# Thirty-six products behind the last one of a two-block network, with stationary columns at several strides

## The chip, the core and the metric

The kernel runs on one core of one Trainium2 chip. The metric is the device time of one launch in microseconds. The kernel before took 952.93 us, the median of three runs (952.01, 952.93 and 953.76).

## What is computed

The reference runs 256 tokens of width 1024 through two layers of one network and one layer of another, all in F32. Each layer of the first is a mixer and a gated feed-forward part, each with a normalisation ahead of it and a sum behind it; the layer of the second has three attention branches, merged by gates, and one last product, which is all that stands near the change:

```python
for i in range(DEPTH):                      # first block, two layers
    h = rms_norm(x, norm_mix[i])
    x = x + mixer(h, ...)                   # convolution and pooling, then sparse attention
    x = x + swiglu(rms_norm(x, norm_ffn[i]), ffn_gate[i], ffn_up[i], ffn_down[i])

# second block, one layer
branches = jnp.stack([o_a * silu(ga), o_b * silu(gb), o_c * silu(gc)], axis=2)
br = jnp.einsum('bsiw,iwd->bsid', branches, w_branch)
merged = jnp.sum(sigmoid(gate_logits) * br, axis=2)
x = x + jnp.einsum('bsd,de->bse', merged, w_out)
```

## The kernel before

Weights come from HBM in tiles of 128 x 2048 F32 values (1 MB), issued by SyncE (SP) into three slots of `raw`. ScalarE rounds each tile into `whi` (line 422, type F32R) and VectorE puts what the rounding left off into `wlo` (line 445). Activations are held in the same two parts (`hhi`/`hlo`, `yhi`/`ylo`: 128 partitions, 8 chunks of 256 columns). One product of F32 values is therefore three products of F32R parts, high by high, high by low and low by high, written out in `product` (lines 464 to 467) and summed in a bank of PSUM. `ps` is PSUM, eight banks of 512 F32 columns. In a row of a profile the first operand behind the arrow is the one that moves, the second the stationary one.

Two helpers set the order in which columns are read. `halves` (line 469) takes n neighbouring columns as two halves and goes to and fro between them, so that each column is half the width away from the one before; `in_order` undoes it when the bank is read:

```python
def halves(columns):
    return columns.rearrange("p (a b) -> p b a", a=2)
```

The gate and up products of the feed-forward part (`ffn_pe`, 256 moving columns) and all products of `rows_part` (line 578, 512 moving columns) move their operand through `halves`; `mm_feature` (256 columns) and the query, key and value products of the second block (512 columns) move theirs in plain order. `place(t, n)` (line 399) is the slot of `whi` or `wlo` that holds tile n, 2048 columns wide.

TensorE (PE) takes its work in program order. The last function in its program is `blk2_pe` (line 2032), which walks an order written out beforehand. Products of the second block rotate through banks 5 to 7 (`bank`, line 2007); `RELEASED` lists, for every use of a bank, the semaphore and the count that tell that ScalarE or VectorE has emptied it. Behind the walk come four tiles of `w_out_2`: for each, PE waits for the tile's low part and for the merged activations, and `mm_rows` (line 600) adds 2 x 2 pieces of 128 tokens x 512 columns into banks 0 to 3, with `yhi`/`ylo` as stationary operand for the first two tiles and `hhi`/`hlo`, chunks 4 to 7, for the last two.

The end of the kernel stands behind that. VectorE adds each finished bank to `x` (line 747). SP stores the first 128 tokens in one DMA (line 2511) and the others in two (line 2514), each as soon as its addition is done, and then waits until all three have landed. Last, every engine drains and a barrier joins all of them; these closing instructions carry line 134. At the start of the kernel PE runs 18 products of a constant tile, plain F32, into bank 7, which nobody reads (line 2695).

Of the kernel before, what the change touches and what calls it, by code (L numbers as in the profile page):

```python
# [21 lines left out]
P = 128  # L22
T = 256
# [108 lines left out]
def build(nc, a, out):  # L132
    ctx = ExitStack()
    with ctx:
        def sb(name, shape, dt=F32):
            return ctx.enter_context(nc.sbuf_tensor(name + "_sb", shape, dt))
# [6 lines left out]
        whi = sb("whi", [P, (SPLIT - 1) * TILE + KC * WIDE], F32R)  # L143
        wlo = sb("wlo", [P, (SPLIT - 1) * TILE + KC * WIDE], F32R)

        x = sb("x", [P, NT, D + 2])
        hhi = sb("hhi", [P, KC, T], F32R)
# [26 lines left out]
        ps = ctx.enter_context(nc.psum_tensor("ps", [P, 8, 512], F32))  # L174
# [224 lines left out]
        def place(t, n):  # L399

            at = (n - N_WIDE - 1) % SPLIT * TILE
            return t[:, at:at + (KC * WIDE if n == N_WIDE else TILE)]
# [66 lines left out]
        def halves(columns):  # L469

            return columns.rearrange("p (a b) -> p b a", a=2)
# [128 lines left out]
        def mm_rows(n, lhs_hi, lhs_lo, k0, first, last, bank=0):  # L600

            for i in range(NT):
                for h in range(2):
                    mm = rows_part(n, lhs_hi, lhs_lo, k0, i, h, first, last, bank)
            return mm
# [1315 lines left out]
        for items, u in segments:  # L1921
# [41 lines left out]
            if u is not None:  # L1963
# [7 lines left out]
                start = JOB_START[u]  # L1971
# [17 lines left out]
                if u == 3:  # L1989
                    k = body.index(("finish", 1))  # L1990
# [9 lines left out]
        N_OUT2 = N_B2 + len(b2_tiles)  # L2000
# [6 lines left out]
        def bank(use):  # L2007
            return 5 + use % 3
# [3 lines left out]
        RELEASED, counts = [], {"emptied": 0, "turned": 0}  # L2012
# [19 lines left out]
        def blk2_pe(pe):  # L2032
            for e in order:
# [64 lines left out]
                elif e[0] == "branch":  # L2098
                    _, b, use = e
                    pe.wait_ge(o_gated, 2 * b + 2)  # L2100
                    for f in range(2):
                        wait_use(pe, use + f)
                        for c in range(2):
                            for i in range(NT):
                                mm = nc.tensor.transpose(
                                    ps[:, bank(use + f), c * T + i * P:c * T + (i + 1) * P],
                                    ob[:, BR_OB[b], i, (2 * f + c) * P:(2 * f + c + 1) * P], ident[:, :])
                        mm.then_inc(b_T, 1)
            for r in range(4):
# [2 lines left out]
                mh, ml = (yhi, ylo) if r < 2 else (hhi, hlo)  # L2112
                mm_rows(N_OUT2 + r, mh, ml, 2 * r + (4 if r < 2 else 0), r == 0, r == 3).then_inc(tile_used, 1)

        BR_OB = (0, 1, 0)

        def qk_index(item):
# [656 lines left out]
```

## Time and profile before

| | |
|---|---|
| median of three runs | 952.93 us (952.01 to 953.76) |
| the profiled execution | 954.75 us |
| its span, first to last instruction | 953.0 us |
| PE busy | 940.2 us (99%), 7053 products |
| PE weight loads | 852.7 us (89%) |
| VectorE busy | 612.3 us (64%) |
| ScalarE busy | 490.8 us (52%) |
| GpSimd busy | 213.7 us (22%) |
| mean granted clock of PE | 0.998 |

The profile is of one execution; its span leaves out what lies ahead of the first instruction and behind the last. PE and its weight loads (PEld) are shown apart, and both overlap: consecutive products start closer together than the time that each of them is shown with, so the distance from start to start is the rate. "q" behind an engine's name marks its queue: waits, drains and DMA issues, which count as no busy time.

### The profile page before, as it was taken

What the parts mean: (1) busy time and instruction counts of PE and PEld (TensorE: products, weight loads), DVE (VectorE), ACT (ScalarE), POOL (GpSimd) and SP (SyncE); (2) the same over time, 40 slices, a digit from 0 to 9 for tenths busy, and PEclk for the clock granted to TensorE, in tenths of its full rate; (3) what the DMA queues carried; (4) which work ended last, traced back from release to release, by engine and by line L of the source; (5) the groups of instructions that cost most, each with busy time, mean ns of one, the idle gap of its engine ahead of it and who ended that gap; (6) DMA issues with size and microseconds to landing.
All of it is one profiled execution on the core that took longest, in us unless ns stands there. A gap on an engine that the chain in (4) does not pass through costs nothing.

```text
span 953.0 us, 17117 instructions
## 1 busy us (share of the span) xinstructions
PE 940.2 (99%) x7053; PEld 852.7 (89%) x7053; DVE 612.3 (64%) x827; ACT 490.8 (52%) x729; POOL 213.7 (22%) x177
## 2 busy tenths in 40 slices
PE   9999999999999998999999999999999999999998
PEld 8999999999889897899999987778787878999997
DVE  5866554545589898764545457756665755946754
ACT  6346444444554565744344446455555555646452
POOL 0005980000032130000000002216472505910100
PEclk9999999999999999999999999999999999999999
DMA  8665856566555512466666574536554525663461
GB/s 275 218 217 164 285 186 210 186 208 205 176 190 169 186 46 89 133 221 191 207 188 208 191 246 147 195 119 207 155 190 126 194 94 175 203 195 98 138 208 45
DMA packets 119636, 168.75 MB, mean 177 GB/s; under 512 B 5556, under 2 KB 88596, under 8 KB 119572
## 3 DMA queue, kind: packets, MB, share of 16 engines
q1 hardware_dynamic: 119140, 167.66, 55.0%
q8 instruction: 45, 0.74, 0.3%
q10 hardware_dynamic: 432, 0.19, 0.1%
q14 instruction: 19, 0.16, 0.1%
HBM read 165.38 MB, written 2.46 MB: 176 GB/s over the span
## 4 chain that ended last, share of the span: by engine, by line
PE 90%; DVE 5%; ACT 2%; POOL 1%; issue 1%; ACTq 0%; DVEq 0%; POOLq 0%
PE ps L465 25%; PE ps L467 24%; PE ps L466 24%; PE ps L923 2%; PE ps L936 2%; DVE wlo_sb L445 2%; PE ps L909 2%; POOL b_inv_sb L2472 1%; PE ps L561 1%; PE ps L734 1%; ACT whi_sb L422 1%; PE ps L500 1%; PE ps L2695 1%; PE ps L574 1%; PE ps L2094 1%
## 5 line engine op out<-in xcount | busy, mean ns | idle before, releaser
L445 DVE TENSOR_TENSOR wlo_sb<-raw_sb,whi_sb 128x2048 fp32r<-128x2048 f32 x143 | 332.7, 2328 | 186.0 <-ACT whi_sb L422 185.9
L422 ACT ACTIVATE whi_sb<-raw_sb 128x2048 fp32r<-128x2048 f32 x143 | 273.7, 1915 | 162.1 <-PE ps L467 145.7
L465 PE MATMUL ps<-hhi_sb,whi_sb 128*128 128x256 f32 x992 | 275.8, 278 | 0.9 <-DVE wlo_sb L445 0.5
L467 PE MATMUL ps<-hhi_sb,wlo_sb 128*128 128x256 f32 x992 | 274.3, 277 | 0.0
L466 PE MATMUL ps<-hlo_sb,whi_sb 128*128 128x256 f32 x992 | 274.3, 276 | 0.0
L465 PEld LDWEIGHTS ps<-hhi_sb,whi_sb 128*128 128x128 f32 x992 | 189.0, 190 | 2.7 <-issue 1.2
L466 PEld LDWEIGHTS ps<-hlo_sb,whi_sb 128*128 128x128 f32 x992 | 189.0, 191 | 0.6
L467 PEld LDWEIGHTS ps<-hhi_sb,wlo_sb 128*128 128x128 f32 x992 | 189.0, 191 | 0.0
L465 PE MATMUL ps<-whi_sb,hhi_sb 128*128 128x512 f32 (+2 forms) x304 | 119.4, 393 | 0.3 <-DVE qkl_sb L2358 0.2
L467 PE MATMUL ps<-whi_sb,hlo_sb 128*128 128x512 f32 (+2 forms) x304 | 116.5, 383 | 0.0
L466 PE MATMUL ps<-wlo_sb,hhi_sb 128*128 128x512 f32 (+2 forms) x304 | 116.4, 383 | 0.0
L465 PE MATMUL ps<-whi_sb,yhi_sb 128*128 128x512 f32 x256 | 97.9, 382 | 1.5 <-DVE wlo_sb L445 0.8
L466 PE MATMUL ps<-wlo_sb,yhi_sb 128*128 128x512 f32 x256 | 97.0, 379 | 0.0
L467 PE MATMUL ps<-whi_sb,ylo_sb 128*128 128x512 f32 x256 | 97.0, 379 | 0.0
L675 POOL TENSOR_TENSOR sinv_sb<-ssum_sb,nhalf_sb 128x1 f32<-128x1 f32 x10 | 6.4, 636 | 387.0 <-ACT scratch_sb L629 386.7
L465 PEld LDWEIGHTS ps<-whi_sb,hhi_sb 128*128 128x128 f32 x304 | 57.2, 188 | 12.8 <-DVE qkl_sb L2358 0.7
L467 PEld LDWEIGHTS ps<-whi_sb,hlo_sb 128*128 128x128 f32 x304 | 57.1, 188 | 12.0
L466 PEld LDWEIGHTS ps<-wlo_sb,hhi_sb 128*128 128x128 f32 x304 | 57.2, 188 | 10.6
L2472 POOL TENSOR_TENSOR b_inv_sb<-b_ss_sb,nhalf_sb 128x16 f32<-128x16 f32 (+1 forms) x10 | 47.5, 4748 | 68.9 <-DVE b_ss_sb L2319 68.9
L465 PEld LDWEIGHTS ps<-whi_sb,yhi_sb 128*128 128x128 f32 x256 | 48.4, 189 | 8.8 <-issue 1.6
L467 PEld LDWEIGHTS ps<-whi_sb,ylo_sb 128*128 128x128 f32 x256 | 48.4, 189 | 6.9
L466 PEld LDWEIGHTS ps<-wlo_sb,yhi_sb 128*128 128x128 f32 x256 | 48.5, 189 | 6.0
(335 smaller groups left out, 1356.1 us busy)
## 6 DMA issues: line engine op xcount, KB each, us to landing
raw_sb<-w_in SPq DMA_DIRECT2D x45, 1024.0 KB, 5.2
raw_sb<-ffn_gate SPq DMA_DIRECT2D x22, 1024.0 KB, 5.3
raw_sb<-ffn_up SPq DMA_DIRECT2D x22, 1024.0 KB, 5.3
raw_sb<-ffn_down SPq DMA_DIRECT2D x22, 1024.0 KB, 5.0
raw_sb<-w_in_even SPq DMA_DIRECT2D x8, 1024.0 KB, 8.4
raw_sb<-w_in_odd SPq DMA_DIRECT2D x8, 1024.0 KB, 5.2
raw_sb<-w_branch SPq DMA_DIRECT2D x6, 1024.0 KB, 5.1
scratch_sb<-bias_rows_dram SPq DMA_DIRECT2D x40, 128.0 KB, 3.2
```

The source lines that it names most:

```text
L422: nc.scalar.activation(place(whi, n0), in_raw(n0), ACT.Copy).then_inc(hi_ready, 1)
L445: nc.vector.tensor_tensor(place(wlo, n0), in_raw(n0), place(whi, n0).bitcast(F32), ALU.subtract).then_inc(lo_ready, 1)
L465: nc.tensor.matmul(dst, l_hi, r_hi, start=first, stop=False)
L466: nc.tensor.matmul(dst, l_hi, r_lo, start=False, stop=False)
L467: return nc.tensor.matmul(dst, l_lo, r_hi, start=False, stop=last)
L500: mm = nc.tensor.matmul(dst, w[:, k, c], h[:, k, :], start=(first and k == 0), stop=(last and k == KC - 1))
L561: nc.tensor.matmul(dst, hhi[:, k0 + k, tok], hi[:, k, :], start=(first and k == 0), stop=False)
L574: mm = nc.tensor.matmul(dst, hlo[:, k0 + k, tok], hi[:, k, :], start=False, stop=stop)
L909: mm = nc.tensor.matmul(ps[:, e, at:at + len(v) * P], ql if part == 2 else qh, kl if part == 1 else kh, start=(part == 0), stop=(part == 2))
L923: mm = nc.tensor.transpose(ps[:, b0 + n % 2, at:at + P], pr[:, 2 * (n % 2) + e, j * P:(j + 1) * P], ident[:, :])
L936: mm = nc.tensor.matmul(ps[q:q + HD, O_BANK, at:at + HD], pT[:, n % 2, e * len(v) + j, q:q + HD], v[j], start=(j == 0), stop=(j == len(v) ...
L2472: nc.gpsimd.tensor_tensor(b_inv[:, nq % 2, :, 0:heads], b_ss[:, nq % 2, 1, :, 0:heads], nhalf[:, 0:2 * heads].rearrange("p (i h) -> p i h" ...
```

## The change

Behind the last of the four `w_out_2` tiles, PE gets three waits, for the last three uses of banks 5 to 7, and 36 products of F32R parts, one pass each, into banks 6 and 7, which nobody reads afterwards. They use what is already on the core: the last tile's `whi` and `wlo`, and `hhi`. Twenty move the 256 columns of chunk 6 of `hhi` through `halves`, four each with 128 stationary columns of `whi` that are neighbours, or 2, 4, 8 and 16 columns apart. Four more do the same with four different runs of neighbours. Then come four pairs: 512 columns, chunks 4 and 5 of `hhi` in turns, and 256 columns of chunk 6. The last four have 128 columns of `hhi` as stationary operand and move 256 columns of `whi`. No semaphore is raised by any of them.

```diff
@@ -2112,6 +2112,22 @@
                 mh, ml = (yhi, ylo) if r < 2 else (hhi, hlo)
                 mm_rows(N_OUT2 + r, mh, ml, 2 * r + (4 if r < 2 else 0), r == 0, r == 3).then_inc(tile_used, 1)
 
+            w, wl = place(whi, N_OUT2 + 3), place(wlo, N_OUT2 + 3)
+            for k in range(1, 4):
+                pe.wait_ge(*RELEASED[-k])
+            h = halves(hhi[:, 6, :])
+            for l in (w[:, 0:P], w[:, 0:2 * P:2], w[:, 0:4 * P:4], w[:, 0:8 * P:8], w[:, 0:16 * P:16]):
+                for _ in range(4):
+                    nc.tensor.matmul(ps[:, 6, 0:T], l, h, start=True, stop=True)
+            for k in range(4):
+                nc.tensor.matmul(ps[:, 6, 0:T], w[:, k * P:(k + 1) * P], h, start=True, stop=True)
+            both = hhi[:, 4:6, :].rearrange("p k t -> p t k")
+            for k in range(4):
+                nc.tensor.matmul(ps[:, 6, :], w[:, k * P:(k + 1) * P], both, start=(k == 0), stop=(k == 3))
+                nc.tensor.matmul(ps[:, 7, 0:T], wl[:, k * P:(k + 1) * P], h, start=(k == 0), stop=(k == 3))
+            for k in range(4):
+                nc.tensor.matmul(ps[:, 6, 0:T], hhi[:, k, 0:P], halves(w[:, 0:T]), start=True, stop=True)
+
         BR_OB = (0, 1, 0)
```

## Rows read from the trace of the kernel before

**Rows 1.** The page: span, PE's busy time, shares of the last chain by engine.

```profile
span 953.0 us, 17117 instructions
...
PE 940.2 (99%) x7053; PEld 852.7 (89%) x7053; DVE 612.3 (64%) x827; ACT 490.8 (52%) x729; POOL 213.7 (22%) x177
...
PE 90%; DVE 5%; ACT 2%; POOL 1%; issue 1%; ACTq 0%; DVEq 0%; POOLq 0%
```

**Rows 2.** The timeline from 942 on, its end: start us, us, engine, line, instruction.

```profile
947.99 0.19 PEld L467 LDWEIGHTS ps<-whi_sb,hlo_sb 128*128 128x128 f32 x1
948.04 1.63 SPq L2514 DMA_DIRECT2D out<-x_sb  x2
948.20 0.38 PE L467 MATMUL ps<-whi_sb,hlo_sb 128*128 128x512 f32 x1
948.61 0.69 DVE L747 TENSOR_TENSOR x_sb<-x_sb,ps 128x512 f32<-128x512 f32 x1 [0.60 <-PE ps L467]
```

**Rows 3.** Instructions of line 134: ns min/median/max, first and last start in us.

```profile
L134 PEldq DRAIN  x1: 4075/4075/4075, 944.5 to 944.5; - x1
...
L134 SPq COMPARE_BRANCH  x1: 38/38/38, 952.6 to 952.6; - x1
L134 SPq DRAIN  x1: 13/13/13, 952.7 to 952.7; - x1
...
L134 PEldq EVENT_SEMAPHORE  x1: 51/51/51, 952.9 to 952.9; - x1
```

**Rows 4.** Waits of SP from 930 on: total us, times, longest us.

```profile
SPq L134 <- DMA out<-x_sb: 2.9, 1, 2.9
```

**Rows 5.** Timeline of 925 to 953: ScalarE's last reading of banks 5 to 7.

```profile
927.89 0.60 ACT L2228 ACTIVATE scratch_sb<-ps 128x512 f32<-128x512 f32 x1 [2.23 <-PE ps L467]
```

**Rows 6.** Timeline of the closing products: first and last of 19 in a row.

```profile
944.10 0.38 PE L466 MATMUL ps<-wlo_sb,hhi_sb 128*128 128x512 f32 x1
...
947.98 0.38 PE L466 MATMUL ps<-wlo_sb,hhi_sb 128*128 128x512 f32 x1
```

**Rows 7.** Timeline of PE in the feed-forward part: first and last of 21.

```profile
149.77 0.28 PE L465 MATMUL ps<-hhi_sb,whi_sb 128*128 128x256 f32 x1
...
152.00 0.28 PE L467 MATMUL ps<-hhi_sb,wlo_sb 128*128 128x256 f32 x1
```

**Rows 8.** Timeline of PE in the first mixer, plain order: first and last of 21.

```profile
39.83 0.28 PE L467 MATMUL ps<-hhi_sb,wlo_sb 128*128 128x256 f32 x1
...
42.18 0.28 PE L466 MATMUL ps<-hlo_sb,whi_sb 128*128 128x256 f32 x1
```

**Rows 9.** Timeline of PE in the second block, plain order: first and last of 15.

```profile
599.63 0.40 PE L467 MATMUL ps<-whi_sb,hlo_sb 128*128 128x512 f32 x1
...
602.90 0.40 PE L466 MATMUL ps<-wlo_sb,hhi_sb 128*128 128x512 f32 x1
```

**Rows 10.** Busy time by stretch: columns as in the first row.

```profile
core 0: us, PE busy (x) PEld busy (x) DVE busy (x) ACT busy (x) POOL busy (x), PEclk, DMA share, GB/s
...
940.00:948.70 8.70, 8.58 (x40) 7.18 (x38) 2.15 (x4) 0.00 (x0) 0.00 (x0) 1.00 0.13 52
```

**Rows 11.** PE's groups by line and form: count, busy us, mean ns, idle before.

```profile
L2695 PE MATMUL ps<-onesd_sb 128*128 128x128 f32 x36 | 7.1, 389 | 1.2 <-POOL onesd_sb L2524 1.2
```

**Rows 12.** Weight loads by line and form: count, busy us, mean ns, idle before.

```profile
L465 PEld LDWEIGHTS ps<-hhi_sb,whi_sb 128*128 128x128 f32 x992 | 189.0, 190 | 2.7 <-issue 1.2 <-DVE wlo_sb L445 0.8
...
L936 PEld LDWEIGHTS ps<-scratch_sb 128*64 128x64 f32 x672 | 22.2, 139 | 7.6 <-issue 5.5 <-ACT scratch_sb L964 0.3
...
L1150 PEld LDWEIGHTS ps<-scratch_sb,onesd_sb 128*128 128x128 f32 x24 | 3.5, 191 | 0.3
...
L1172 PEld LDWEIGHTS ps<-raw_sb,scratch_sb 128*32 128x32 f32 x64 | 1.7, 109 | 1.1
...
L1238 PEld LDWEIGHTS ps<-scratch_sb 128*15 128x15 f32 x8 | 0.4, 95 | 0.1
```

**Rows 13.** DMAs that write the output: time from issue to landing.

```profile
DMA to landing us min/median/max: 2.1/2.7/3.2
```

## Prediction

> **What bounds the kernel now.** First the page: TensorE (PE) is busy 99% of a span of 953.0 us and the chain that ended last is 90% PE [rows 1]. That alone would say that every product added to PE is paid in full. But the change stands behind the last product, so I read the end of the timeline next [rows 2]: the last product starts at 948.20 and takes 0.38, so PE is done at 948.58; VectorE's last addition runs from 948.61 to 949.30; the last store is issued right behind it. Then the closing instructions, line 134 [rows 3]: every engine drains, and a barrier joins them. PE's drain is entered at 944.5 and lasts 4.075 us, so it ends at 948.6, with the last product. SyncE (SP) reaches its own drain only at 952.7, because it waits 2.9 us for the last store to land [rows 4]; the barrier then runs to 953.0. So over the last 4.1 us (948.6 to 952.7) PE has nothing to do and the store sets the end. That slack is the cover of the change: PE work added behind the last product is free up to 4.1 us, and what exceeds it moves the end one for one.
>
> **The change part by part.** Nothing is removed or moved. Added are three waits and 36 products, each with its own weight load, all on PE, with no semaphore and no reader.
>
> *The waits.* They ask that the last three uses of banks 5 to 7 have been emptied. The last instruction that signals this is ScalarE's copy of line 2228, at 927.89 for 0.60 us [rows 5], 20 us before the last product, so none of them stands. Their own handling costs nothing either: PE's sequencer is at its drain 4 us before the last product ends [rows 3], so it works through waits while products queued ahead still run. Behind them on PE only the new products are queued; nobody waits for those but the closing barrier.
>
> *The products.* 28 move 256 columns in the interleaved order of `halves` (20 with stationary columns at strides 1, 2, 4, 8, 16, four each; 4 with plain neighbours; 4 with hhi as stationary); the 4 pairs move 512 columns, with the two feature chunks interleaved, and 256. Start to start, not the 0.28 or 0.38 us of a row, is the price, since rows overlap. In the closing products, 512 interleaved columns go at one per 215.6 ns (18 steps in 3.88 us [rows 6]); in the feed-forward stage, 256 interleaved columns at one per 111.5 ns (20 steps in 2.23 us [rows 7]), with stationary neighbours. So 28 x 111.5 = 3.12 us, and 4 x (215.6 + 111.5) = 1.31 us, together 4.43 us. The bound below is columns alone: 213 and 107 ns at 2.4 columns per ns (512 columns in 215.6 ns is that rate), 4.27 us. If all of them went as moving columns read in plain order do, 117.5 ns for 256 [rows 8] and 233.6 for 512 [rows 9], it would be 4.69 us. I take 4.43, because the moving operands of the change are interleaved as in rows 6 and 7. The granted clock is 1.0 up to the last product [rows 10], and the new products follow without a gap, so I take the full level, 2.4 GHz.
>
> *Each is one pass.* A product of plain F32 operands, like the 18 unread warm-up products of line 2695, leaves 36 rows [rows 11]; those of lines 465 to 467 leave one row each. The new ones have F32R operands. The 36 rows also show that unread products are run.
>
> *The stationary strides.* No row of before shows a stationary operand at a stride. Loads are recorded with 95 ns for 15 columns, 109 for 32, 139 for 64 and 191 for 128 [rows 12]: about 0.85 ns a column, 109 ns for 128, over a fixed part of some 82 ns. One load starts with every product, 111.5 ns apart, though each is recorded with 190: they overlap one another by that fixed part. So a load needs about the time in which 256 columns are moved, and there is little room: a stride that slows the load shows at once. Bound below: nothing, the strided load stays behind the product before it as the others do. Bounds above, from the recorded 190 ns: if strided loads follow one another without overlap, a product costs 190 instead of 111.5 ns; for 12 products at strides 4 to 16 that is 0.94 us, for 16 at strides 2 to 16 1.26 us. If they don't run behind the products either, 190 ns come on top of 111.5, 3.04 us for 16. I take zero, by the one pair of rows that shows an operand read with jumps: `halves` jumps 128 or 256 elements at every column and is the faster form, 215.6 against 233.6 ns for 512 columns [rows 6, 9], so a jump by itself is no cost where PE reads its moving operand.
>
> The Trainium skill (SBUF — State Buffer, section "Door 1: The DMA port swizzle") speaks against that: it says that reads are served in lines of 16 bytes, four F32 values, that full bandwidth wants at least two hits on a line, and that every crossing pays. By that rule strides 4, 8 and 16 would pay and stride 2 would not; an estimate by that page alone, half the rate for one hit where two are wanted, makes a load 220 ns and the 12 products 1.3 us dearer. For moving operands the rows disagree as far as jumps go, interleaved being faster than plain, but interleaving alternates between two runs of neighbours and a stride of 16 never comes back; no run here shows the load's side yet.
>
> *Sum.* PE ends 4.43 us later, at 948.58 + 4.43 = 953.01, 0.3 us past the 952.7 at which SP is ready now; the barrier behind it is as long as before, so the span becomes 953.3. The profiled execution took 954.75, 1.75 more than its span and 1.82 more than the median of 952.93; I carry the difference over: 954.75 + 0.3 for the profiled one, 952.93 + 0.3 = 953.2 for the median.
>
> **The rivals.**
> First, the cover is thinner without a profile. The last store lands after 3.2 us, while the others land after 2.1 and 2.7 [rows 13]. If the normal landing is one of these, PE's end is passed by 0.8 to 1.4 us instead of 0.3: 953.7 to 954.3. For it: the spread; against: it is the last one in the only trace there is.
> Second, strided loads take longer, since each column is read without its neighbours, so that they follow one another at their recorded length: 190 ns a product, 0.94 us more if strides 4 to 16 are concerned, 1.26 if 2 to 16: 954.2 to 954.5. For it: the load has no time to spare; against: the jumps of `halves` cost nothing. The page named above has this as its rule, for strides from 4 on.
> Third, and on the slower side: strided loads don't run behind the product before them. Each then costs its whole 190 ns [rows 12] on top of the 111.5: 16 products at strides 2 to 16, 3.04 us, 956.3. It decides (over 0.2%, 1.9 us) from (1.9 - 0.3) / 16 = 0.10 us a product. For it: nothing in the trace rules it out, as no strided load is there; against: the load of the last closing product starts at 947.99, 0.21 us ahead of it [rows 2], so pulling ahead is the normal course, whatever the addresses.
> Fourth, the products are dropped or cost less than the cover: 952.9. Against: the warm-up rows, and the 4.27 us that columns alone need.
>
> **How the numbers follow.** Forecast 0.60 (953.2); cover thinner 0.12 (954.0); longer loads 0.17 (954.4); unhidden loads 0.10 (956.3); dropped 0.01. 0.2% of 952.93, about what a measurement can tell from no change, is 1.9 us: 951.0 and 954.8 are the limits. The first two cases and the last lie inside; of the longer loads, whose upper end is 0.3 us short of the limit, I count 0.05 beyond; so slower 0.15, faster 0.02 (the spread of the three runs is 1.75 us), same 0.83. Range: from 952.3, the forecast less half that spread, to 955.0, which takes in both ends of the longer loads with 0.5 us for the spread; it leaves out the third rival, 0.10, and little else.
>
> **What would show it.** After: 36 more PE rows, all with one pass; the 256-column ones 0.11 us apart at every stride, pairs 0.33; PE's drain ending near 953.0 and SP's at 952.7, so that PE is the last into the barrier; a clock of 1.0 to the end; nothing changed ahead of 948. If rows at strides 4, 8 and 16 stand 0.19 us or more apart, the second rival holds; if those from stride 2 on stand 0.3 apart, the third. The forecast falls if the 36 take over 6.0 us (4.1 of cover and 1.9).

## The result and the profile after

The changed kernel took 955.45 us (median of 7 runs, 954.86 to 956.88) against 952.93 us of the kernel before in the same comparison: ratio 1.0028, 95% interval 1.0017 to 1.0039. A second comparison (`e10_after_again`, below) gave 1.0021, 1.0012 to 1.0030. Forecast were 953.2 us and a range up to 955.0: the time lies above the range.

The closing instructions of the profile after, in the columns of [rows 3], show who comes last into the barrier now:

```profile
L134 SPq DRAIN  x1: 13/13/13, 951.9 to 951.9; - x1
L134 PEldq DRAIN  x1: 2810/2810/2810, 952.0 to 952.0; - x1
```

PE's drain ends at 952.0 + 2.81 = 954.9, SP's at 951.9: the two have changed places, as the forecast said, but PE is later than the forecast 953.0 by 1.9 us. Of these, 0.3 us come from ahead of the change: the last closing product ends at 948.92 here and ended at 948.58 before. SP's waits after (line, what for, total us, times, longest us) say the same from the other side:

```profile
SPq L134 <- PEq L134: 3.2, 1, 3.2
...
SPq L134 <- DMA out<-x_sb: 1.7, 1, 1.7
```

SP waits 1.7 us for the last store (2.9 before, [rows 4]) and then 3.2 us for PE. The timeline of PE after (start us, us, engine, line, instruction, count; neighbours of one line are merged) has the added work:

```profile
948.54 0.38 PE L467 MATMUL ps<-whi_sb,hlo_sb 128*128 128x512 f32 x1
948.76 3.88 PE L2121 MATMUL ps<-hhi_sb,whi_sb 128*128 128x256 f32 x20
952.47 0.61 PE L2123 MATMUL ps<-hhi_sb,whi_sb 128*128 128x256 f32 x4
952.92 0.38 PE L2126 MATMUL ps<-hhi_sb,whi_sb 128*128 128x512 f32 x1
953.14 0.27 PE L2127 MATMUL ps<-hhi_sb,wlo_sb 128*128 128x256 f32 x1
...
954.23 0.61 PE L2129 MATMUL ps<-whi_sb,hhi_sb 128*128 128x256 f32 x4
```

The last closing product ends at 948.92, the last added one at 954.84: 5.92 us, not 4.43. All of the difference is in line 2121, the twenty with strides: 952.47 - 948.76 = 3.71 us where 20 x 111.5 ns = 2.23 were forecast, 1.48 us more. The four behind it take 0.45 (112 ns each), a pair 0.33, as forecast. The instructions of that one line (ns min/median/max) show the loads:

```profile
L2121 PEld LDWEIGHTS ps<-hhi_sb,whi_sb x20: 189/316/337, 948.5 to 952.1; 128*128 128x128 f32 x20
L2121 PE MATMUL ps<-hhi_sb,whi_sb x20: 273/385/404, 948.8 to 952.2; 128*128 128x256 f32 x20
```

189 ns is the old load [rows 12]; the median is 316. So the second rival happened, with longer loads than it had been given. The granted clock stays at 1.00 meanwhile (third column from the end; busy time by stretch, columns as in [rows 10]), so the clock has no part in it:

```profile
948.90:954.90 6.00, 5.94 (x37) 5.64 (x35) 0.69 (x1) 0.00 (x0) 0.00 (x0) 1.00 0.29 110
```

### The profile page after: what moved, and what is told of

The parts are those of the page before. It is cut to its first block, busy times and chain, and to the rows that moved or that the text cites. A ratio compares the mean times of both kernels' runs of the same rounds, so it can differ in the third digit from the quotient of the medians.

```text
span 955.1 us, 17190 instructions
## 1 busy us (share of the span) xinstructions
PE 944.7 (99%) x7089; PEld 857.1 (90%) x7089; DVE 612.3 (64%) x827; ACT 490.7 (51%) x729; POOL 216.0 (23%) x177
## 4 chain that ended last, share of the span: by engine, by line
PE 89%; DVE 5%; ACT 2%; POOL 1%; DMA 1%; issue 1%; SPq 0%; ACTq 0%; DVEq 0%
PE ps L465 24%; PE ps L467 24%; PE ps L466 24%; PE ps L923 2%; PE ps L936 2%; DVE wlo_sb L445 2%; PE ps L909 2%; POOL b_inv_sb L2488 1%; DMA raw_sb<-w_in_even 1%; PE ps L561 1%; ACT whi_sb L422 1%; PE ps L500 1%; PE ps L734 1%; PE ps L574 1%; PE ps L2094 1%
```

## Experiments

Executions of one and the same kernel differ by over 3 us here, with the granted clock (last section) and with how the kernel ends (`e8_before_again` and on). Beside the ratios, which take all of them, this table has medians of the executions recorded with a mean granted clock of 1.000, count in brackets, each against the kernel before in its own comparison.

| kernel | work behind the last closing product | ratio (95%) | clock 1.000 | before, clock 1.000 | difference |
|---|---|---|---|---|---|
| e1_neighbours | 4.43 us | 1.0002 (0.9993 to 1.0011) | 953.52 (6) | 952.84 (6) | +0.7 |
| e2_under_cover | 2.23 us | 0.9992 (0.9983 to 1.0001) | 952.06 (4) | 952.84 (6) | -0.8 |
| e6_twice | 11.85 us | 1.0080 (1.0065 to 1.0096) | 961.14 (3) | 952.84 (6) | +8.3 |
| e7_ahead | none, 5.9 us ahead of it | 1.0046 (1.0031 to 1.0062) | 957.95 (2) | 952.84 (6) | +5.1 |
| e9_four | 0.44 us | 0.9992 (0.9983 to 1.0001) | 951.97 (5) | 952.46 (6) | -0.5 |
| e10_after_again | 5.92 us | 1.0021 (1.0012 to 1.0030) | 955.14 (8) | 952.46 (6) | +2.7 |
| e11_one | 0.11 us | 0.9992 (0.9983 to 1.0000) | 951.85 (8) | 952.77 (15) | -0.9 |
| e12_ten | 1.11 us | 1.0000 (0.9991 to 1.0008) | 952.05 (4) | 952.77 (15) | -0.7 |

**e1_neighbours: the strides undone.**

```diff
-            for l in (w[:, 0:P], w[:, 0:2 * P:2], w[:, 0:4 * P:4], w[:, 0:8 * P:8], w[:, 0:16 * P:16]):
+            for l in (w[:, 0:P], w[:, P:2 * P], w[:, 2 * P:3 * P], w[:, 3 * P:4 * P], w[:, 4 * P:5 * P]):
```

> The 20 strided loads are replaced by loads of 128 neighbours (five places of the tile, four products each); everything else of the change stays. In the trace of the changed kernel the 36 products end 5.9 us after the last closing product, with 0.11 us at stride 1, 0.12 at 2 and 0.22 to 0.24 at 4, 8 and 16. Theory (strides 4 to 16 cost 12 x 0.12 us, and the store's landing leaves a cover of some 3 to 3.5 us): the 36 end 4.45 us after the last closing product, and the time falls by 1.4 to 1.5 us, to about 954.0. Rival (the strides are not what costs, the end is late for another reason, as more instructions or three waits): the time stays at 955.4. If the cover were the 4.1 us that the forecast read: 953.2.

PE's timeline:

```profile
946.64 0.38 PE L467 MATMUL ps<-whi_sb,hlo_sb 128*128 128x512 f32 x1
946.86 2.39 PE L2121 MATMUL ps<-hhi_sb,whi_sb 128*128 128x256 f32 x20
949.09 0.61 PE L2123 MATMUL ps<-hhi_sb,whi_sb 128*128 128x256 f32 x4
...
950.84 0.61 PE L2129 MATMUL ps<-whi_sb,hhi_sb 128*128 128x256 f32 x4
```

The twenty take 949.09 - 946.86 = 2.23 us, and all 36, from the end of the last closing product (947.02) to their own (951.45), 4.43, the forecast sum to the hundredth. The ratio of 1.0002 can't be told from no change, and its interval, up to 1.0011, lies below both of the changed kernel's, from 1.0017 and 1.0012. So the strides are what made the kernel measurably slower; without them the time can't be told from the forecast, a ratio of 1.0003.

**e3_512_columns: strided loads ahead of longer products.** Four products each with strides 1, 2, 4, 8 and 16, all moving 512 interleaved columns.

```diff
+            for _ in range(4):                        # in place of the 36; the same for each stride
+                nc.tensor.matmul(ps[:, 6, :], w[:, 0:4 * P:4], both, start=True, stop=True)
```

> 20 products that move 512 interleaved columns, with stationary columns at strides 1, 2, 4, 8 and 16, four each, in place of the 36. Theory (a strided load takes 0.22 to 0.24 us but runs behind the product before it): 0.216 us from start to start at strides 1 and 2, 0.22 to 0.24 at 4 to 16. Rival (a strided load doesn't overlap the product, or adds its 0.12 us to any product): 0.33 to 0.34 us at strides 4 to 16.

The timeline, one line of the kernel for each stride:

```profile
946.88 1.03 PE L2121 MATMUL ps<-hhi_sb,whi_sb 128*128 128x512 f32 x4
947.75 1.03 PE L2123 MATMUL ps<-hhi_sb,whi_sb 128*128 128x512 f32 x4
948.61 1.11 PE L2125 MATMUL ps<-hhi_sb,whi_sb 128*128 128x512 f32 x4
949.55 1.13 PE L2127 MATMUL ps<-hhi_sb,whi_sb 128*128 128x512 f32 x4
950.52 1.08 PE L2129 MATMUL ps<-hhi_sb,whi_sb 128*128 128x512 f32 x4
```

From group to group a product costs 217 ns at stride 1, 215 at 2, 235 at 4 and 242 at 8; behind the first one at stride 16 the next starts 227 ns later. So a strided load still runs behind the product before it; the distance is the longer of the two, and ahead of 512 columns nearly all of it is hidden. The third rival of the prediction is out.

**e4_sweep: which strides, and the load by itself.** Six products each in place of the 36:

```diff
+                nc.tensor.matmul(ps[:, 6, 0:T], w[:, 0:3 * P:3], h, start=True, stop=True)      # strides 1, 2, 3, 4, 5, 6, 12, 16
+                nc.tensor.matmul(ps[:, 6, 0:HD], w[:, 0:4 * P:4], halves(hhi[:, 6, 0:HD]), start=True, stop=True)  # 1, 2, 4, 16
+                nc.tensor.matmul(ps[:, 6, 0:T], hf[:, 0:4 * P:4], halves(w[:, 0:T]), start=True, stop=True)
```

> Six products each, in place of the 36: 256 interleaved moving columns with stationary strides 1, 2, 3, 4, 5, 6, 12 and 16; then 64 moving columns with strides 1, 2, 4 and 16, so that the load alone sets the rate; then stationary columns at stride 4 from hhi instead of whi. Theory (four F32 neighbours come with one read, about 1.85 ns each, and 128 columns need 128 x stride / 4 of them up to one per column): 0.11 us at stride 1, 0.118 at 2, 0.176 at 3, 0.22 to 0.24 from 4 on, whatever the stride; with 64 moving columns the same 0.118 at 2 and 0.22 to 0.24 at 4 and 16; hhi as whi. Rival (strides that are powers of two meet one bank of the memory): 0.11 to 0.13 us at 3, 5 and 6 and more at 12 and 16 than at 4.

The timeline; lines 2121 to 2135 are strides 1, 2, 3, 4, 5, 6, 12 and 16, lines 2137 to 2143 strides 1, 2, 4 and 16 with 64 moving columns:

```profile
947.80 0.83 PE L2121 MATMUL ps<-hhi_sb,whi_sb 128*128 128x256 f32 x6
948.47 0.88 PE L2123 MATMUL ps<-hhi_sb,whi_sb 128*128 128x256 f32 x6
949.18 1.21 PE L2125 MATMUL ps<-hhi_sb,whi_sb 128*128 128x256 f32 x6
950.23 1.57 PE L2127 MATMUL ps<-hhi_sb,whi_sb 128*128 128x256 f32 x6
951.64 1.52 PE L2129 MATMUL ps<-hhi_sb,whi_sb 128*128 128x256 f32 x6
953.00 1.50 PE L2131 MATMUL ps<-hhi_sb,whi_sb 128*128 128x256 f32 x6
954.33 1.77 PE L2133 MATMUL ps<-hhi_sb,whi_sb 128*128 128x256 f32 x6
955.93 1.49 PE L2135 MATMUL ps<-hhi_sb,whi_sb 128*128 128x256 f32 x6
957.26 0.75 PE L2137 MATMUL ps<-hhi_sb,whi_sb 128*128 128x64 f32 x6
957.85 0.87 PE L2139 MATMUL ps<-hhi_sb,whi_sb 128*128 128x64 f32 x6
958.55 1.58 PE L2141 MATMUL ps<-hhi_sb,whi_sb 128*128 128x64 f32 x6
959.95 1.49 PE L2143 MATMUL ps<-hhi_sb,whi_sb 128*128 128x64 f32 x6
961.25 1.75 PE L2145 MATMUL ps<-whi_sb,hhi_sb 128*128 128x256 f32 x6
```

A sixth of the distance to the next start: 112 ns at stride 1, 118 at 2, 175 at 3, 235 at 4, 227 at 5, 222 at 6, 267 at 12, 222 at 16. From stride 2 to 4 the cost follows the number of groups of four F32 neighbours that the 128 columns touch: 64 at stride 2, 96 at 3, 128 at 4, about 1.83 ns each (118 / 64 = 1.84, 175 / 96 = 1.82, 235 / 128 = 1.84). From 4 on each column has a group of its own, and the cost stays at 222 to 235 ns, powers of two or not; as strides 3, 5 and 6 pay, the rival is out. Stride 12 is out of line (267, or 2.09 a group), and why is open. That groups of four are what is read is inferred from these distances. With 64 moving columns it is 117, 233 and 217 ns at strides 2, 4 and 16, as with 256, and at stride 1 98 in the mean (31 for the first step, whose load had run behind a longer product, then 111 to 112): the load alone sets the rate. The last line has hhi at stride 4 as stationary operand; behind a first step of 374 ns its starts are 233 to 238 apart, as with whi.

**e5_moving: the same on the moving side.** 256 columns of whi at strides 1, 2, 4, 8, then 256 neighbours taken to and fro between 2, 4 and 8 parts, stationary neighbours throughout.

```diff
+                nc.tensor.matmul(ps[:, 6, 0:T], w[:, 0:P], w[:, 0:4 * T:4], start=True, stop=True)          # strides 1, 2, 4, 8
+                nc.tensor.matmul(ps[:, 6, 0:T], w[:, 0:P], w[:, 0:T].rearrange("p (a b) -> p b a", a=8), start=True, stop=True)  # 2, 4, 8
```

> Six products each, in place of the 36, all with 128 neighbours of whi as stationary columns: 256 moving columns of whi at strides 1, 2, 4 and 8, then 256 neighbours taken as 2, 4 and 8 parts between which the order goes to and fro. Theory (the moving operand is read in the same groups of four, 1.85 ns each, but a few groups stay at hand, which is why to and fro between two parts is free): 0.118 us at stride 1, 0.24 at 2, 0.47 at 4 and 8; 0.11 in two parts. In 4 and 8 parts 0.11 if that many groups are kept, 0.47 if only two are. Rival (only stationary loads suffer from strides): 0.11 to 0.12 us throughout.

```profile
947.77 0.88 PE L2120 MATMUL ps<-whi_sb 128*128 128x256 f32 x6
948.49 1.52 PE L2122 MATMUL ps<-whi_sb 128*128 128x256 f32 x6
949.84 1.58 PE L2124 MATMUL ps<-whi_sb 128*128 128x256 f32 x6
951.23 1.49 PE L2126 MATMUL ps<-whi_sb 128*128 128x256 f32 x6
952.54 0.85 PE L2128 MATMUL ps<-whi_sb 128*128 128x256 f32 x6
953.23 1.01 PE L2130 MATMUL ps<-whi_sb 128*128 128x256 f32 x6
954.07 1.50 PE L2132 MATMUL ps<-whi_sb 128*128 128x256 f32 x6
```

120 ns at stride 1, 225 at 2, 232 at 4, 218 at 8; 115 in two parts (111 within the group), 140 in four, (1.50 - 0.40) / 5 = 220 in eight. Both theories are off: strides do cost the moving operand (the rival falls), but strides 4 and 8 cost no more than 2, half of the 0.47 us that one group of four for each column would have given. What holds for the argument of the prediction: interleaving of two parts is free, of eight parts it isn't. So jumps aren't free in general. That `halves` is free because it comes back to each group at once fits these numbers, but is argued, not shown: four parts come back too, if later, and pay a part.

**e2_under_cover, e6_twice, e7_ahead: the cover.** Twenty products with neighbours only; all 36 run twice; all 36 put ahead of the last `w_out_2` tile.

```diff
+            for k in range(20):                       # e2, in place of the 36
+                nc.tensor.matmul(ps[:, 6, 0:T], w[:, k % 16 * P:(k % 16 + 1) * P], h, start=True, stop=True)
+            for _twice in range(2):                   # e6, around the 36
+                if r == 3:                            # e7, the 36 ahead of mm_rows of the last tile
```

> Only 20 products of 256 columns with neighbours as stationary columns are left of the 36, 2.23 us of PE behind the last closing product. Theory (the last store covers some 3 us or more): the time is that of the kernel before, 952.9, within 0.2%, and PE's drain ends ahead of SP's. Rival (any work behind the last product costs its length, or longer code costs): 955.1.

> The 36 products run twice, 72 in all. Theory (beyond the cover PE is the last into the barrier and each us costs one us): 5.9 us more than the changed kernel, 961.3, with the second 36 as long as the first. Rival (the cover is used a second time, or the granted clock changes): less than 960 or more than 963.

> The same 36 products, with their waits, stand ahead of the last w_out_2 tile instead of behind it, so that no store covers them. Theory: all of their 5.9 us are paid, 952.9 + 5.9 = 958.8, and the difference to the changed kernel (955.45) is the cover, 3.4 us. Rival (there is no cover, the changed kernel is slow for its 2.5 us of strided loads alone): 955.4.

Twice the work costs 8.3 us more than before at clock 1.000, 5.6 more than once (2.7; by the medians of all executions 961.17 - 955.24 = 5.9), for 5.93 us of products: beyond the cover each us is paid. That there is cover, `e2_under_cover` shows directly: PE's drain ends at 949.4, SP's at 950.1. Subtracting what is paid from what is added gives the cover in the timed executions: 11.85 - 8.3 = 3.55, 5.92 - 2.7 = 3.2, and from e1 4.43 - 0.7 = 3.7. So it is 3.2 to 3.7 us, where the trace of before shows 4.1. `e7_ahead` pays 5.1 of its 5.9 us, and `e2_under_cover` is 0.8 below the kernel before, both 0.8 less than expected. (At clock 1.000 `e7_ahead` has two executions only.) The next experiments tell what they have in common.

**e8_before_again, e9_four, e11_one, e12_ten: the last store.** The kernel before once more, and 4, 1 and 10 products in place of the 36.

```diff
+            for k in range(4):                        # e9; one in e11, range(10) in e12
+                nc.tensor.matmul(ps[:, 6, 0:T], w[:, k * P:(k + 1) * P], halves(hhi[:, 6, :]), start=True, stop=True)
```

> The kernel before, unchanged, for a second profile of its end. In its first profile the last store landed 3.2 us after its issue, in the changed kernel's 2.0 us, though nothing of the store differs. Theory (the landing varies from one execution to the next, and 3.2 us was a late one): 2.0 to 2.7 us here, and 2.9 to 3.6 us from the end of the last product to SP's drain. Rival (products that run while the store lands make it faster): 3.2 us again, and 4.1 us to SP's drain.

> Only four products of 256 columns with neighbours are left of the 36, 0.45 us of PE behind the last closing product. In the two profiles of the kernel before, a transfer of 16 KB of instructions runs while the last store does (950.12 to 951.10 in the first) and the store lands after 3.1 to 3.2 us; in the changed kernel and all its variants so far that transfer came at 943 to 946, ahead of the stores, and the store lands after 2.0. Theory (PE's code is fetched in pieces, the piece that is due at the very end delays the last store by 1.1 us, and a few more instructions make it due earlier): the fetch comes ahead of the stores, the store lands after 2.0 us, the span is 1.1 us shorter than before, ratio 0.9988. Rival (the length of the products behind the end, not the number of instructions, decides): landing 3.1 to 3.2 us and ratio 1.0000.

> One single product of 256 columns with neighbours is left of the 36, two instructions of PE and the three waits. With four products the fetch of instructions came 3.8 us ahead of the last store's issue and the store landed after 2.0 us. Theory (any few instructions more make the last piece due while PE still works): fetch ahead of the stores, landing after 2.0 us, ratio 0.9988. Rival (one product is too few): the fetch runs beside the last store, landing 3.1 to 3.2 us, ratio 1.0000.

> Ten products of 256 columns with neighbours, 1.1 us of PE behind the last closing product, to settle the time of the earlier landing: four and twenty products both gave 0.9992 with 1.0000 still inside the interval. Theory: landing after 2.0 us, span 1.1 us shorter, ratio 0.9988, and below 1.0000 by the interval. Rival (the body of the kernel gives the 1.1 us back): 1.0000.

DMA queues while the last store lands (queue, kind, packets, MB, share; in the last row KB and us from issue to landing). The kernel before, from 949 to 953:

```profile
q1 hardware_dynamic: 280, 0.50, 33.8%
q8 instruction: 1, 0.02, 1.5%
out<-x_sb SPq DMA_DIRECT2D x1, 256.0 KB, 3.2
```

`e8_before_again`, from 948 to 951.6:

```profile
q8 instruction: 1, 0.02, 2.1%
...
out<-x_sb SPq DMA_DIRECT2D x1, 256.0 KB, 3.1
```

The changed kernel, from 948.9 to 955:

```profile
q1 hardware_dynamic: 337, 0.66, 28.4%
out<-x_sb SPq DMA_DIRECT2D x1, 256.0 KB, 2.0
```

In both profiles of the kernel before, one transfer of 16 KB of instructions runs beside the last store, which lands after 3.1 to 3.2 us. In the changed kernel, both times, and in its ten other variants no such transfer stands there, and the store lands after 2.0, with PE busy meanwhile or not (in `e7_ahead` it is idle). So `e8_before_again` has its rival's numbers (3.1 us, and 4.0 from the last product to SP's drain), but not for its rival's reason: it isn't the products that matter but where the fetch falls. In `e9_four` and `e12_ten` it starts ahead of the stores (947.4 and 945.2), in `e11_one`, against what was expected, only at 951.1, behind the landing and even behind the last instruction (949.9); the store is quick in either case.

The packets show the delay itself. From 1.67 us behind the issue of the last store on, this is left in the kernel before (951 to 953) and in the changed kernel (951.34 to 953):

```profile
q1 hardware_dynamic: 9, 0.02, 3.3%
```

```profile
DMA packets 0, 0.00 MB, mean 0 GB/s; under 512 B 0, under 2 KB 0, under 8 KB 0
```

These nine packets are 16 of the store's 256 KB. The first starts at 951.09, where the fetch (950.12 to 951.10) ends, and they run one after another to 952.1; all others are through at 951.0. In `e8_before_again` the fetch ends at 949.69 and nine such packets run from 949.68 to 950.7. So a sixteenth of the store waits for the fetch, and that is the 1.1 us.

In time the other place of the fetch is worth 0.5 to 0.9 us at clock 1.000 in the four kernels whose products the store covers (e2, e9, e11, e12), less than the 1.1 expected. Their ratios, three times 0.9992 and once 1.0000 (`e12_ten`, its rival's), don't settle it by themselves.

The spans of the timed executions, first to last instruction, tell more. At clock 1.000 the kernel before has a median span of 950.2 us in 27 executions, and so have e2, e9 and e12, whose profiles show a store that lands after 2.0. The shortest spans of e2, e9, e11 and e12 are 949.8 to 950.0; with a store 1.1 us later the kernel before would not come below 950.9, and 20 of its 27 do. So in most executions of the kernel before the last store isn't late. Instead more time passes outside the span: device time less span is 1.75 to 2.01 us in the changed kernel and in e1, e2, e6, e7, e9 and e12, and over 2.01 in 32 of 65 executions of the kernel before, up to 3.01. The one profile with a fetch behind the last instruction, that of `e11_one`, has 2.41. So the fetch seems to cost the kernel before either beside the store or behind the end; for the executions without a profile that is argued, not shown. With 0.7 us for it, `e7_ahead` adds up: 5.9 less 0.7 are 5.2, measured 5.1.

**e10_after_again: the changed kernel timed once more**, without an edit.

> The changed kernel as it is, timed again beside the kernel before on one chip, for a tighter interval. Theory (the kernel before ends with the late store, 4.1 us after its last product, and PE now ends 5.9 us after it): 1.8 us more, ratio 1.0019. Rival (the cover is the 3.0 us that a store landing after 2.0 us would leave): 2.9 us more, ratio 1.0030.

The interval, 1.0012 to 1.0030, holds both the theory (1.0019) and the rival (1.0030). At clock 1.000 the difference is 2.7 us in time and 3.1 in span (953.3 against 950.2), nearer to the rival's 2.9 than to the theory's 1.8. The work behind the end is the same to a hundredth (5.92), so by the spans the cover is 2.8 us, about what a store landing after 2.0 leaves: in the profile of `e12_ten` SP's drain starts 2.9 us behind the end of the last closing product.

## Why the prediction was wrong

Much was right, by the runs. PE has cover behind its last product and becomes the last into the barrier. The waits cost nothing: the first added product starts 0.22 us behind the last closing one. Each product is one pass (7089 rows of PE on the page after, 36 more than [rows 1], so the fourth rival is out too) and follows without a gap at the full clock, 2.4 GHz. The sum with neighbours throughout, 4.43 us, was measured as 4.43 (`e1_neighbours`, ratio 1.0002).

The step that failed is "I take zero" for the stationary strides. It measured 1.48 us: 12 products at strides 4 to 16 cost 0.22 to 0.24 us instead of 0.11, the four at stride 2 0.12. The mechanism was the second rival, given 0.17. Two arguments misled. `halves` was taken as evidence that jumps are free; `e5_moving` shows that this holds for two interleaved parts only, and that a moving operand at a stride doubles too. And the rival's bound, 190 ns, was the length of the old load, an overlapped length that says nothing of how long a strided one takes; loads turned out at up to 337 ns, 0.22 to 0.24 us apart.

The Trainium skill (SBUF — State Buffer, section "Door 1: The DMA port swizzle"), which the prediction weighed and set aside, had the direction: strides of 4 and more pay and 2, with two hits on a line, doesn't, and the estimate made from it, 220 ns and 1.3 us, was nearer than the row-based bound. The trace agrees for stationary columns (118 ns at stride 2, 235 at 4) and differs for moving ones, where stride 2 already takes 225 ns against 120.

The second step that failed is the cover. The prediction read 4.1 us from one execution, in which a fetch of instructions held up the last store, and carried the 1.75 us between its time and its span over to all others. The spans at clock 1.000 say that most executions of the kernel before have no such late store and a cover of 2.8 us. In time 3.2 to 3.7 us are left of the 4.1, as the kernel before spends more outside its span. So the first rival was right about the landing, which is 2.0 us where no fetch runs beside the store; its price, 0.5 to 1.1 us above the forecast, was about paid, by 0.4 to 0.9. [rows 13] spoke for it more than was said: the 2.7 there belongs to the store of 512 KB, and the only other store of 256 KB, the size of the last one, landed after 2.1.

The terms add up. With the covers of `e1_neighbours` and `e6_twice` (3.7 and 3.55), 0.3 forecast, 1.5 for strides and 0.4 to 0.55 for the cover make 2.2 to 2.4 us, and 2.5 and 2.7 were measured; the rest is within the intervals. The range ended at 955.0 because each rival was put beside the forecast alone. Two of them with separate causes can come together: 953.2 + 1.3 + 1.1 = 955.6 would have been an honest upper end.

## What to carry to other kernels

A weight load counts as soon as it is longer than the product before it: with 256 moving columns the load of 128 neighbouring F32R columns is just as long (112 ns), so a stride there is paid at once, and 512 moving columns hide nearly all of it. Before calling an access pattern free by analogy, ask whether the row that you lean on uses every neighbour that it fetches. Work behind the last product is free only up to the landing of the last store, and that landing can hold something that has nothing to do with the store. A profile tells this of one execution: compare its span with the spans of the others before taking a wait of it as the rule.

## What the runs showed of the hardware

The granted clock of the same stretch differs between executions. Busy time by stretch of the kernel before, of `e10_after_again` and of `e9_four`, the third column from the end being the granted clock:

```profile
361.30:364.50 3.20, 2.16 (x10) 2.19 (x11) 3.17 (x6) 0.66 (x2) 0.00 (x0) 0.63 0.03 5
364.50:368.00 3.50, 2.92 (x39) 2.40 (x39) 1.81 (x5) 3.21 (x6) 0.00 (x0) 0.85 0.71 218
```

```profile
361.30:364.50 3.20, 2.20 (x34) 1.99 (x36) 3.02 (x6) 1.54 (x4) 0.00 (x0) 1.00 0.02 5
364.50:368.00 3.50, 2.92 (x27) 2.53 (x24) 3.13 (x8) 2.08 (x4) 1.11 (x1) 1.00 0.81 255
```

```profile
361.30:364.50 3.20, 2.40 (x12) 2.42 (x12) 3.07 (x6) 0.66 (x2) 0.00 (x0) 0.50 0.02 5
364.50:368.00 3.50, 3.46 (x37) 2.79 (x36) 1.88 (x6) 3.12 (x6) 0.00 (x0) 0.50 0.76 236
```

Just ahead, from 356.0 to 361.3, PE was busy for 3.2 to 3.5 of 5.3 us in all three. In one execution the clock then stays at 2.4 GHz, in another it is at 1.2 GHz for part of the 6.7 us, in the third for all of it. In the comparisons of `e1_neighbours`, `e9_four` and `e11_one` the kernel before took 951.8 to 953.5 us in 27 executions at a mean clock of 1.000 and 952.8 to 955.1 in 38 below it, medians 952.69 and 954.05. That 1.4 us is as large as the effect under study, and comparing at one clock is what separated its terms.

Weight loads at a stride of 16 don't follow that clock. In `e4_sweep` it fell while products of 64 columns ran, by the busy time of two stretches of it:

```profile
948.00:957.40 9.40, 9.40 (x50) 9.40 (x49) 0.69 (x1) 0.00 (x0) 0.00 (x0) 1.00 0.17 66
959.00:961.40 2.40, 2.40 (x12) 2.40 (x12) 0.00 (x0) 0.00 (x0) 0.00 (x0) 0.50 0.00 0
```

The loads behind 959.95, at 1.2 GHz, stand 217 ns apart, those behind 955.93, at 2.4 GHz, 222.
